# Mixture-of-experts loop: the order of VectorE's gate-times-up against the weight remainders, and of TensorE's h transposes against the next rows

## What is computed

```python
idx, wts = top 8 of 64 experts for every row
for each expert e:
    rows = x[tokens of e]                                     # (count, 1024)
    h = silu(rows @ w_gate[e]) * (rows @ w_up[e])             # (count, 256)
    y[tokens of e] += (h @ w_down[e]) * weight
```

## Time and profile before

| | us |
|---|---|
| median of three executions | 1954.76 |
| profiled execution, its own time | 1955.29 |
| its span, first to last instruction | 1953.4 |
| TensorE busy in the span | 1765.9 (90%) |
| VectorE / ScalarE / GpSimd busy | 939.4 / 783.1 / 461.1 |
| mean granted TensorE clock | 0.952 |

### The profile page before, as it was taken

One profiled execution on the slowest core, in us unless ns is written; L12 is line 12 of the kernel. 1 busy time (PEld: TensorE's weight loads), 2 busy tenths in 40 slices (PEclk: granted clock), 3 DMA queues, 4 the chain that ended last, 5 costly groups with the idle time before them and its releaser, 6 DMA issues. The chain is left out here.

```text
span 1953.4 us, 26454 instructions
## 1 busy us (share of the span) xinstructions
PE 1765.9 (90%) x7450; PEld 1139.1 (58%) x7451; DVE 939.4 (48%) x1603; ACT 783.1 (40%) x1451; POOL 461.1 (24%) x594
## 2 busy tenths in 40 slices
PE   7999999975996999899999998999999999866997
PEld 4666666533785666666666666665666666543443
DVE  2333333311675543554444555454545535537885
ACT  2222222211330554564555555555556545541221
POOL 0010000000673232223323323233233232210110
PEclk9999999976997999899999998999999999887999
DMA  9200000125122687887878788878888887868651
GB/s 356 76 0 0 0 0 0 34 75 172 34 56 77 215 276 216 279 262 228 257 242 244 240 244 266 250 226 250 255 254 272 253 239 213 279 189 339 253 188 38
DMA packets 159129, 358.81 MB, mean 184 GB/s; under 512 B 32002, under 2 KB 46146, under 8 KB 156509
## 3 DMA queue, kind: packets, MB, share of 16 engines
q1 hardware_dynamic: 123125, 285.79, 47.8%
q0 software_dynamic: 35328, 72.27, 10.4%
q10 hardware_dynamic: 640, 0.28, 0.1%
HBM read 330.19 MB, written 68.98 MB: 204 GB/s over the span
## 5 line engine op out<-in xcount | busy, mean ns | idle before, releaser
L194 DVE TENSOR_TENSOR lo_gu<-raw_gu,hi_gu 128x1024 fp32r<-128x1024 f32 x260 | 317.4, 1226 | 519.9 <-ACT hi_gu L188 517.0
L1242 PE MATMUL B<-raw_d,hT 128*128 128x512 f32 (+1 forms) x768 | 361.1, 621 | 53.2 <-ACT hT L1353 33.7
L188 ACT ACTIVATE hi_gu<-raw_gu 128x1024 fp32r<-128x1024 f32 x260 | 274.6, 1061 | 177.2 <-PE B L1192 177.1
L1192 PE MATMUL B<-hi_gu,x_hi 128*128 128x512 f32 (+1 forms) x768 | 327.2, 426 | 0.0
L1087 POOL DMA_INDIRECT y_dram<-y,put x128 | 136.4, 1066 | 715.1 <-issue 359.7
L1192 PE MATMUL B<-hi_gu,x_lo 128*128 128x512 f32 (+1 forms) x768 | 303.5, 395 | 0.0
L1192 PE MATMUL B<-lo_gu,x_hi 128*128 128x512 f32 (+1 forms) x768 | 302.5, 394 | 0.0
L1242 PEld LDWEIGHTS B<-raw_d,hT 128*128 128x128 f32 (+1 forms) x768 | 136.7, 185 | 236.8 <-issue 190.1
L1339 ACT ACTIVATE y<-B 128x512 f32<-128x512 f32 (+1 forms) x256 | 146.8, 595 | 215.1 <-PE B L1242 190.9
L1192 PEld LDWEIGHTS B<-hi_gu,x_hi 128*128 128x128 f32 (+1 forms) x768 | 135.3, 176 | 56.3 <-issue 13.2
L1192 PEld LDWEIGHTS B<-lo_gu,x_hi 128*128 128x128 f32 (+1 forms) x768 | 135.6, 177 | 54.7 <-issue 13.8
(11 more groups left out here) (220 smaller groups left out, 1785.2 us busy)
## 6 DMA issues: line engine op xcount, KB each, us to landing
raw_gu<-in_w_exp_gate SPq DMA_DIRECT2D x264, 256.0 KB, 4.6
raw_gu<-in_w_exp_up SPq DMA_DIRECT2D x264, 256.0 KB, 5.6
raw_d<-in_w_exp_down SPq DMA_DIRECT2D x65, 1024.0 KB, 6.6
yk<-y_dram SPq DMA_DIRECT2D x16, 2048.0 KB, 11.9
rows_dram<-ple SPq DMA_DIRECT2D x9, 512.0 KB, 2.6
w_big<-in_w_in SPq DMA_DIRECT2D x2, 2048.0 KB, 12.5
w_out<-in_w_out SPq DMA_DIRECT2D x1, 4096.0 KB, 18.3
w_big<-in_w_ple_gate SPq DMA_DIRECT2D x64, 64.0 KB, 6.2
```

Of the source, the lines that this page charges most:

```text
L188: act.activation(part_of(keep["hi_gu"], i), part_of(keep["raw_gu"][buf], i), ACT.Copy).then_inc(keep["hi_set"], 1)
L194: dve.tensor_tensor(part_of(keep["lo_gu"], i), part_of(keep["raw_gu"][buf], i), part_of(keep["hi_gu"], i).bitcast(F32), ALU.subtract).then ...
L1192: ins = pe.matmul(out, lhs[x], rhs[w], start=first and i == 0, stop=last and i == 2)
L1242: ins = pe.matmul(Y[half][0:BLK[b], :], hT[:, f, b * P:b * P + BLK[b]], raw_d[:, f, half * 512:(half + 1) * 512], start=(f == 0), stop=(f ...
```

## The change

VectorE takes the third weight remainder quarter from before `hidden` to behind the row parts; the fourth stays last. TensorE transposes three quarters of the next rows, then h, then the last quarter, then `down`. The first transposes of the round are as before. The order of SyncE's, ScalarE's and GpSimd's instructions stays.

```diff
-            def transposes(j, b, gathered):
-
-                pe.wait_ge(rows_ld[b], 32 * gathered)
-                pe.wait_ge(x_lo_ev, 4 * j + 1)
-                for i in range(4):
+            def transposes(j, b, gathered, parts):
+
+                if 0 in parts:
+                    pe.wait_ge(rows_ld[b], 32 * gathered)
+                    pe.wait_ge(x_lo_ev, 4 * j + 1)
+                for i in parts:
...
             def expert(r, q, n, b, blocks):
                 m, j, after_b = r * E + n, r * NJ + n, (b + 1) % 2
                 gate_up(m, j, blocks)
-                transposes(j + 1, after_b, ROWS_USED[after_b] * r + q + b + 1)
+                transposes(j + 1, after_b, ROWS_USED[after_b] * r + q + b + 1, (0, 1, 2))
                 h_transposes(m, blocks)
+                transposes(j + 1, after_b, ROWS_USED[after_b] * r + q + b + 1, (3,))
                 down(m, blocks)
...
             def expert(r, n, b):
                 m = r * E + n
-                for i in range(PARTS - 1):
+                for i in range(PARTS - 2):
                     split_lo(dve, keep, (b + 1) % 2, m + 1, i)
                 hidden(m, 0)
                 hidden(m, 1)
                 for i in range(4):
                     x_part(r * NJ + n + 1, i)
-                split_lo(dve, keep, (b + 1) % 2, m + 1, PARTS - 1)
+                for i in range(PARTS - 2, PARTS):
+                    split_lo(dve, keep, (b + 1) % 2, m + 1, i)
                 own_e.clear()
```

More of the change, by code:

```diff
@@ L1268, in one_round @@
                 pe.wait_ge(idx_set, 2 * r + 2)
-                transposes(r * NJ, 0, ROWS_USED[0] * r + 1)
+                transposes(r * NJ, 0, ROWS_USED[0] * r + 1, range(4))
                 with pe.Fori(0, E // 2) as q:
```

## The result

The changed kernel takes 1980.31 us (median of 6 executions, 1976.89 to 1985.13) against 1955.89 us of the kernel before in the same runs: ratio 1.013, 95% interval 1.0104 to 1.0156. It is slower by about 25 us. The profiled execution took 1980.69 us, its span 1978.8, which is 25.4 more than before.

The account below looks back on a forecast made before the run. TensorE was taken as the bound on average, with transfers close behind. The terms -1.6 - 3.4 - 1.7 - 2.8 + 3.8 + 1.7 = -4.0 took 1955.3 to 1951.3 us, range 1943 to 1968 us.

Parts of the forecast that it names:

- the clock: Second experts of pairs: one more wait for down weights ends in slow down matmuls, costing 1.7 us (0 to 6.7).
- the longer runs: Three or four one-block experts in a row: first experts gain 1.7 us, experts with late rows 2.8 us.
- the second expert of a pair: Second of two one-block experts in a row: down weights land 0.76 us later; five pairs cost 3.8 us (0 to 12.2).
- two-block expert ahead: One-block expert behind a two-block one: quarters later, but SyncE issues down weights only after the last down; cost nothing.
- the slack ahead of the late rows: Three or four one-block experts in a row: the loads' delay falls into time before late rows, no cost counted.
- Two-block expert: Expert of two blocks: h transposes start earlier, gain 0.05 us each (0 to 0.10), 1.6 us over 32 experts.
- One-block expert, nothing late: Expert of one block without late rows: multiplies and h transposes start earlier, gain 0.42 us; 3.4 us in eight singles.
- Other waits: GpSimd's next gather: it follows its own scatter, later than the quarter transposed about 0.4 us late; no cost counted.
- rival A: Pairs pay nothing since the queue drains when it drains; two-block gain full 0.10 us each; 1944.2 us, chance 0.26.
- Rival B: Third quarter's bytes delay down weights: pairs 2.44 us each, slow clock in all five, no two-block gain; 1966.3 us, chance 0.17.
- three signs of being wrong: In the new trace: two-block experts gaining several tenths, down-weight waits behind two-block experts, or a later gather.
- rival C: In one-block experts h comes no earlier, so the 0.42 us gain is missing; 1956.4 us, chance 0.11.

Follow-up runs that it names:

- after_down_ahead34: The changed kernel, but SyncE issues the down weights ahead of the third and fourth quarters' loads; 38 us less of time than the changed kernel.
- behind_hidden: The changed kernel with both moves, but VectorE's third remainder directly behind the two multiplies, ahead of the row parts; 1955.80 us, ratio 0.9994.
- late_load: The kernel before, but SyncE holds the third quarter's load back until the fourth remainder is done; 1991.59 us, ratio 1.0172.

## Why the prediction was wrong

The prediction summed to 4.0 us of gain, and the profiled execution took 25.4 us more. Of these 29.4 us the pairs make 14.9 (worked out at +5.5 with the clock, measured +20.4) and the longer runs 15.3 (worked out at -4.5, measured +10.8). So what failed is the step on *the second expert of a pair*, and with it *two-block expert ahead*, whose late quarters I put at nothing: the landing was taken at 0.76 us and was 1.8 to 1.9 where it could be read, the clock at 1.7 us and was 5.2, late rows have no term in the pairs and cost 10.5, and the sentence that in the runs the delay falls into the slack ahead of the late rows does not hold. What TensorE spent in each place, changed less before (us, added up from the two traces):

```
                        waits for   waits for      waits for h    own time
                        rows        down weights   and its copy   of TensorE
two-block experts         +0.4          0.0           -9.2          +5.9
single one-block           0.0         +1.2           -3.7          -0.1
pairs                    +10.5         +5.0           -2.6          +7.4
runs of three or four     +8.8         +9.5           -4.0          -3.5
```

TensorE's own time grows where the granted clock is lower and where the row transposes stand in two pieces. The waits for rows grew more than those for down weights, 19.7 us against 15.7.

**Two-block expert: right.** Worked out 0.05 us each, 1.6 in all; the h transposes start 0.12 us earlier, about 0.07 of it is left in the expert's time, and the sum is 2.9 us, of which 1.0 is the first expert of the loop. The reason was right too: h is now what TensorE waits for.

**One-block expert, nothing late: right in mechanism and size.** 0.42 us, seen as 1.97 to 1.55 us between the transposes. Eight singles gave 2.6 instead of 3.4 us, since two of them, right behind a two-block expert, now wait 0.5 and 0.7 us for down weights.

**The second expert of a pair: in three pairs the late landing that I named, but the term too small, and the bytes ahead of it wrong.** I allowed 0 to 2.44 us for the landing and took 0.76, the delay at issue. It was near the upper end. The pair of the earlier trace rows, before:

```profile
1309.05 3.70 PE L1242 MATMUL B<-raw_d,hT 128*128 128x512 f32 x8 [0.61 <-ACT hT L1353]
1313.33 0.38 SPq L993 DMA_DIRECT2D raw_d<-in_w_exp_down  x1
```

and changed, second expert:

```profile
1331.45 5.79 PE L1243 MATMUL B<-raw_d,hT 128*128 128x512 f32 x8 [4.46 <-DMA raw_d<-in_w_exp_down]
```

From the first expert's down to the second's it was 13.65 us (1309.05 to 1322.70) and is 15.97 (1315.48 to 1331.45). Of the 2.32 more, 0.42 is the first expert's gain given back. The rest, 1.9, lies in the landing: the issue came 0.6 later, from there to the down 10.69 us pass instead of 9.37. In two other pairs the same sum gives 1.9 and 1.8.

In the two pairs that are left the second expert waits for its rows, 2.25 us in one; in the other it is the largest loss of the five, 7.3 of the 20.4 us:

```profile
1508.92 2.38 PE L1203 MATMUL B<-ident,rows 128*128 128x128 f32 x12 [8.24 <-DMA rows<-rows_dram,now]
```

Under *Other waits* I had seen that the gather follows GpSimd's own scatter, but put no delay on the scatter. No rival had one either.

Why the lower end of the landing did not hold is seen in the transfers ahead of it. In the stretch of 3.5 us from 10.5 us after the first gate-up matmul of the pair of the earlier trace rows, they run short, 234 GB/s instead of 343 (changed and, below it, before; last columns: granted clock, share of the DMA engines, GB/s):

```profile
1317.50:1321.00 3.50, 3.50 (x13) 2.19 (x12) 1.95 (x2) 2.37 (x6) 2.28 (x2) 1.00 0.76 234
```

```profile
1310.60:1314.10 3.50, 3.50 (x13) 2.04 (x12) 1.37 (x2) 2.08 (x5) 0.00 (x0) 1.00 0.93 343
```

But over the whole way from the pair's first gate-up matmul to the second expert's down matmuls they do not, here changed and, below it, before:

```profile
1307.00:1331.40 24.40, 19.60 (x94) 14.82 (x92) 16.58 (x24) 16.84 (x29) 6.69 (x6) 0.95 0.93 301
```

```profile
1300.10:1322.70 22.60, 19.69 (x95) 14.76 (x93) 15.47 (x23) 16.54 (x29) 5.50 (x6) 1.00 0.89 292
```

The engines are no less busy than before, and move 7.3 MB on this way instead of 6.6. In the two other pairs it is 7.6 MB instead of 7.0 and 7.3 instead of 7.0, at a share of 0.94 each, before 0.94 and 0.93. At 300 GB/s that is an estimated 1.1 to 2.5 us, for a landing that is 1.8 to 1.9 later. So the queue did stay full on the whole; what failed is my sentence that the same bytes stand ahead of the down weights. What came in is seen in the two-block expert ahead of the pair: the load of its third quarter was issued 9.5 us ahead of the pair's first gate-up matmul (1300.13) and is now issued 3.7 us ahead of it (1307.00), before and changed:

```profile
1290.61 0.33 SPq L182 DMA_DIRECT2D raw_gu<-in_w_exp_gate  x1
1303.26 0.33 SPq L182 DMA_DIRECT2D raw_gu<-in_w_exp_gate  x1
```

In `after_down_ahead34`, where both late quarters stand behind the down weights, 6.2 MB are moved on this way, and the down weights are not waited for. The Trainium skill's rule on rings ("DMA: Bandwidth & Descriptors", Queues, rings and completion order), on which rival A stood, says in what order one ring's work is taken; it says nothing on how much work stands in it, and that is what changed here.

**The clock: the term mis-sized.** The second expert's eight down matmuls took 5.79 us instead of 3.67. The stretch around them, granted clock 0.63:

```profile
1331.40:1337.20 5.80, 5.75 (x9) 2.54 (x10) 0.00 (x0) 0.60 (x1) 3.42 (x5) 0.63 0.82 238
```

I counted one more fall, at 1.67 us, with a range to 6.7. In this pair the 1.9 us of landing brought 2.1 us of clock; over the second experts of all five pairs the down matmuls took 5.2 us more than before. In the changed trace every one of the six waits for down weights of over 4 us was followed by down matmuls of 5.28 to 5.90 us, once 6.44; before, the longest such wait was 2.9. The length of the wait alone does not decide it: of the waits of 2.1 to 2.9 us in the five pairs before, one was followed by slow down matmuls, of those of 2.3 to 3.7 us in `behind_hidden` all five.

Rival B's price for the pairs was 12.2 + 6.7 = 18.9 us, and 20.4 was measured. That these lie close is luck: about half of the 20.4 are waits for rows, which B does not have.

**The runs of three and four: wrong.** I wrote that the same delay falls into the slack ahead of the late rows, and booked 4.5 us of gain. They lost 10.8: the waits for down weights grew by 9.5 us and those for rows by 8.8. The slack is not fixed, because rows depend on GpSimd's scatters, and these run beside the loads. One case of it: after the two-block expert ahead of the pair GpSimd's first scatter and its next, before:

```profile
1298.72 1.04 POOL L1087 DMA_INDIRECT y_dram<-y,put  x1 [10.06 <-ACT y L1339]
1303.96 1.42 POOL L1087 DMA_INDIRECT y_dram<-y,put  x1 [4.20 <-issue]
```

and changed:

```profile
1305.59 1.03 POOL L1087 DMA_INDIRECT y_dram<-y,put  x1 [7.59 <-ACT y L1341]
1312.65 0.96 POOL L1087 DMA_INDIRECT y_dram<-y,put  x1 [6.03 <-issue]
```

The second scatter waits for the first to land, and starts 7.06 us after it instead of 5.24; the gather behind it is as much later. So the step "two-block expert ahead: I cost it at nothing" failed as well. Its cover, SyncE's wait for the last down, holds the issue of the down weights but not the landing of the scatter, beside which the two late quarters now run, nor that of the down weights: four one-block experts right behind a two-block one wait for these, 0.4 to 0.9 us, where before none did. Waits behind two-block experts and a later gather are two of the three signs of being wrong that the prediction named. That the scatters are late by the late load is borne out by `late_load`; by how much the time of the runs would fall if the rows alone were in time was not tried.

**Rival A** fell with the pairs, **rival C** by the timeline: the multiply starts right behind the sigmoid. **Rival B** named one mechanism of the two, but as the less likely case, and without the runs and the late rows.

## What to carry to other kernels

An instruction that frees a buffer is also the start of a transfer. When it is moved, price the transfer's new place in the queue: what is issued right behind it, what deadline that has, and into which later stretch its bytes now fall, the next expert's included. Here 4 us of delay for 512 KB with a deadline more than an expert away cost 1.5 to 1.7%, because a 1 MB load with a near deadline stood behind it, and scatters ran beside it. Issuing that load first, with TensorE's move and the third remainder behind the multiplies, made the kernel 1% faster than before; a little under half of that (0.45%) is the new order in the queue alone, without any move.

A stretch in which the queue is full, here 0.9 busy, becomes longer with every load that is pushed into it from ahead: that it stays full says nothing on when its last load lands. A slack that was read from one trace is not fixed when what fills it, here the scatters, shares the transfers that are moved. And a wait that grows past what the trace has shown so far may bring a second price, here the clock.

## What was not expected of the hardware

GpSimd's small copy ahead of its scatter (L1095, 128x2) takes 0.20 us at the median, but 2.41 in the timeline of the changed one-block expert above, from 1317.08, beside VectorE's two remainders, which run from 1317.10 for 2.35 us. Its mean, before and changed, over the expert loop:

```profile
L1095 POOL COPY put<-y_at 128x2 int32 (+1 forms) x63 | 18.8, 299 | 0.6
```

```profile
L1095 POOL COPY put<-y_at 128x2 int32 (+1 forms) x61 | 37.8, 619 | 0.6
```

The Trainium skill ("SBUF — State Buffer", Who interferes with whom) says that a GpSimd instruction that reads the SBUF and a VectorE instruction with two inputs from the SBUF contend for a shared port pair, which is locked and not divided. The copy and the remainder are such instructions, and the trace agrees: the copy ends within 0.1 us of the second remainder. Two remainders back to back act as one long lock, where before each stood alone and the longest copy of this line took 1.23 us, beside one remainder of 1.23.

In the expert above the time is not on the path, since the scatter that follows waits for ScalarE's y. In the pair with the 8.24 us it is, ahead of the gather that TensorE waited for:

```profile
1493.06 2.35 DVE L194 TENSOR_TENSOR lo_gu<-raw_gu,hi_gu 128x1024 fp32r<-128x1024 f32 x2
1493.41 2.03 POOL L1077 COPY now<-idx 128x2 int32 x1
```

It does not explain the loss: over all 64 experts the copies of L1077 take 21.0 us, against 26.8 before.
